# Mixture-of-experts stage: four experts at a time on 32-column tiles, in fixed order, with eight weight buffers

## What is computed

```python
N_GROUPS, EXPERTS_PER_GROUP, TOP_K, D_EXPERT = 4, 8, 2, 512
g_top_p, g_top = lax.top_k(softmax(xt @ router_group_w + router_group_b), 1)      # one group of 8 experts a token
e_logits = (xt @ router_expert_w + router_expert_b).reshape(n, 4, 8)
e_top_logit, e_top = lax.top_k(e_logits[group of the token], TOP_K)               # two experts in that group
gates = g_top_p * softmax(e_top_logit)
# for each of the token's two experts e:
hdn = silu(x @ w_gate[e]) * (x @ w_up[e])      # w_gate, w_up: 1024 x 512
y  += gate * (hdn @ w_down[e])                 # w_down: 512 x 1024
```

## Time and profile before

| | us |
|---|---|
| median of 3 runs | 2416.12 (2413.78 to 2418.14) |
| span of the profiled execution | 2417.7 |
| PE busy / weight loads / DVE / ACT / POOL | 2155.3 / 1491.3 / 746.5 / 406.8 / 186.7 |
| HBM read, written | 440.29 MB, 1.05 MB |
| mean granted TensorE clock | 0.946 |

### The profile page before, as it was taken

How to read it: one execution, slowest core, us unless ns; L and a number is a source line. 1 busy time by engine, 2 the same in 40 slices (tenths; PEclk the granted TensorE clock), 3 DMA queues, 4 the chain that set the end, 5 groups by cost and what they waited for, 6 DMA issues and landing times.

```text
span 2417.7 us, 21513 instructions
## 1 busy us (share of the span) xinstructions
PE 2155.3 (89%) x8282; PEld 1491.3 (62%) x8282; DVE 746.5 (31%) x1215; ACT 406.8 (17%) x868; POOL 186.7 (8%) x157
## 2 busy tenths in 40 slices
PE   3904999989999789999899998878999999999997
PEld 2403868777888457688788885566444444444443
DVE  4887423642232445236422233322000000000001
ACT  1112322202110242312121101331001001001001
POOL 0560300000000274000000000000000000000000
PEclk9956999999999899999999999977999999999998
DMA  7512624244446464342554465003987886886881
GB/s 270 178 69 70 207 93 153 105 163 152 148 165 226 135 231 173 106 139 105 174 166 147 144 244 172 35 1 116 335 297 247 294 307 244 296 295 244 309 294 71
DMA packets 224588, 442.54 MB, mean 183 GB/s; under 512 B 10421, under 2 KB 59765, under 8 KB 224501
## 3 DMA queue, kind: packets, MB, share of 16 engines
q1 hardware_dynamic: 221557, 440.08, 52.1%
q10 hardware_dynamic: 2944, 1.28, 0.2%
HBM read 440.29 MB, written 1.05 MB: 183 GB/s over the span
## 4 chain that ended last, share of the span: by engine, by line
PE 81%; DVE 8%; DVEq 3%; ACT 3%; issue 2%; SPq 1%; DMA 1%; ACTq 0%
PE acc L660 29%; PE acc L1092 18%; PE aux L1109 9%; PE acc L670 5%; PE acc L935 3%; PE aux L935 3%; PE acc L957 3%; PE aux L602 3%; DVE biasm L1563 2%; DVEq L1564 2%; PE acc L1038 1%; SPq L530 1%; ACT area L1144 1%; PE aux L624 1%; DVE gates L1560 1%
## 5 line engine op out<-in xcount | busy, mean ns | idle before, releaser
L660 PE MATMUL acc<-hT,ring 128*128 128x256 f32 x2688 | 594.8, 383 | 6.9 <-ACT hT L1217 6.9
L660 PEld LDWEIGHTS acc<-hT,ring 128*128 128x128 f32 x2688 | 515.3, 192 | 82.5 <-ACT hT L1217 7.7
L1092 PE MATMUL acc<-ring,area 128*128 128x512 f32 x1024 | 450.7, 594 | 3.7 <-ACT area L1144 1.9
L1092 PEld LDWEIGHTS acc<-ring,area 128*128 128x128 f32 x1024 | 192.7, 191 | 234.6 <-issue 232.7
L1109 PE MATMUL aux<-ring,area 128*128 128x512 f32 x512 | 225.4, 593 | 2.7 <-ACT area L1144 2.7
L2120 DVE SCALAR_TENSOR_TENSOR area<-area,acc 128x512 f32<-128x512 f32 x32 | 23.9, 748 | 600.0 <-PE acc L1092 600.0
L602 PE MATMUL aux<-kc,area 128*128 128x128 f32 (+2 forms) x473 | 76.7, 310 | 130.2 <-DVE area L1676 54.2
L670 PE MATMUL acc<-ring,hT 128*128 128x512 f32 (+1 forms) x384 | 167.5, 596 | 12.1 <-ACT hT L1217 12.1
L1109 PEld LDWEIGHTS aux<-ring,area 128*128 128x128 f32 x512 | 97.0, 190 | 124.2 <-issue 120.5
L602 PEld LDWEIGHTS aux<-kc,area 128*128 128x128 f32 (+2 forms) x473 | 64.3, 158 | 157.9 <-DVE area L1676 54.3
L1500 POOL TENSOR_TENSOR zb<-ring,cact 128x512 f32<-128x512 f32 x80 | 90.0, 1130 | 750.3 <-DMA ring<-in_ada_w 740.2
(11 more groups left out here) (318 smaller groups left out, 1804.5 us busy)
## 6 DMA issues: line engine op xcount, KB each, us to landing
ring<-in_w_in SPq DMA_DIRECT2D x34, 2048.0 KB, 8.9
ring<-in_w_gate SPq DMA_DIRECT2D x32, 2048.0 KB, 8.3
ring<-in_w_up SPq DMA_DIRECT2D x32, 2048.0 KB, 8.3
ring<-in_w_down SPq DMA_DIRECT2D x32, 2048.0 KB, 7.9
ring<-in_ada_w SPq DMA_DIRECT2D x28, 2048.0 KB, 9.1
ring<-in_ffn_w_up SPq DMA_DIRECT2D x44, 1024.0 KB, 7.5
ring<-in_ffn_w_down SPq DMA_DIRECT2D x10, 2048.0 KB, 8.0
ring<-in_w_out SPq DMA_DIRECT2D x6, 2048.0 KB, 7.8
```

What stands on the lines that cost most here:

```text
L660: mm = pe.matmul(acc[LU.buf[use]][:, SEQ * j:SEQ * j + SEQ], w[:, k, c0:c0 + P], x[:, k, :], start=(k == 0), stop=(k == n - 1))
L1092: mm = pe.matmul(acc[e % 2][:, DE * i:DE * i + DE], xg[:, k, :], w[:, k, :], start=(k == 0), stop=(k == KT - 1))
```

## The change

- An expert has 32 slots (`CAP`) of its own, a token has two (one for each of its experts). Four experts make a *quad*: their 4 x 32 slots fill 128 columns. PE computes the four on four column tiles: each matmul has 32 stationary columns and writes 32 partitions, and the loop runs over the four experts inside the loop over k. The matmuls of an expert run only over its own slots.
- Eight quads instead of four groups. Seven run unrolled, in fixed order; the eighth and every further pass for a quad with an expert of over 32 tokens (`overflow_table`, up to 1 + 16 passes) run in a loop whose passes and quads are read from `meta`. Each such pass loads all 12 matrices of its quad.
- Weights have eight 2 MB buffers (`slots8`: the four of `ring`, `gates` and three pieces of `area`). Eight loads are issued during the second attention. Each further load waits until the matmuls of the matrix eight before it have ended (`spent`).
- Loads put 8 (gate, up) or 4 (down) consecutive rows of a matrix on a partition, one row of 16 KB, where they put rows of 2 or 4 KB. `h2t` and `he` are copied in that order of features.
- The gate weight moves from DVE's product into the scatter matrix (`pw`). Gather, scatter and turns of neighbouring quads are placed between the batches.
- `va2`, `h2t`, `xg`, `ygs`, `fin`, `hs`, `he`, `heT` and the router's small tiles get other places, and the squares of the last two norms go to `sqx2` and `sqx3`.

```diff
-PASS_CHUNKS = ["e_g0", "e_u0"] + [...]
+W_SLOTS = 8
+RING_OF = (None, 3, 0, None, None, None, 1, 2)
+QUAD_CHUNKS = 3 * QE
+STATIC = (QUADS - 1) * QUAD_CHUNKS
+LOOP_STEP = QUAD_CHUNKS + 4
...
...
# SP
+            def expert_source(quad, c):
+                w = a[("w_gate_2", "w_up_2", "w_down_2")[c // QE]]
+                return w[0, bass.ds(quad * QE + c % QE, 1)].rearrange("e (p k) n -> p (e k n)", p=P)
+            def expert_load(n):
+                sp.dma_start(slots8[n % W_SLOTS], expert_source(n // QUAD_CHUNKS, n % QUAD_CHUNKS)).then_inc(expert_in[n % W_SLOTS], 16)
...
+                if name == "m_kb":
+                    expert_load(0)
+            mid_done("m_kb", 2)
+            expert_load(1)
+            mid_done("m_vb", 2)
+            expert_load(2)
+            sp.wait_ge(t2_out, 4)
+            expert_load(3)
+            sp.wait_ge(oT_out, 2)
+            expert_load(4)
+            expert_load(5)
+            mid_done("m_wo0", 4)
+            expert_load(6)
+            mid_done("m_wo1", 4)
+            expert_load(7)
+            for n in range(W_SLOTS, STATIC):
+                sp.wait_ge(spent, n - W_SLOTS + 1)
+                expert_load(n)
             sp.wait_ge(routed, 1)
+            passes = sp.value_load(meta[0:1, 0:1], min_val=1, max_val=1 + OVER)
+            with sp.Fori(0, passes) as i:
+                quad = sp.value_load(meta[0:1, bass.ds(i + 1, 1)], min_val=0, max_val=QUADS - 1)
+                for c in range(QUAD_CHUNKS):
+                    sp.wait_ge(spent, i * LOOP_STEP + (STATIC + c - W_SLOTS + 1))
+                    s = (STATIC + c) % W_SLOTS
+                    sp.dma_start(slots8[s], expert_source(quad, c)).then_inc(expert_in[s], 16)
...
# PE
+            def hidden(c0, b, dst, full_of):
+                for e in range(QE):
+                    full_of(c0 + e)
+                for k in range(KT):
+                    for e in range(QE):
+                        w = shaped(slots8[(c0 + e) % W_SLOTS], KT, DE)
+                        mm = pe.matmul(dst[CAP * e:CAP * e + CAP, :], xg[:, b, k, CAP * e:CAP * e + CAP], w[:, k, :],
                                        start=(k == 0), stop=(k == KT - 1))
+                        if k == KT - 1:
+                            mm.then_inc(spent, 1)
+            def down(c0, full_of, extra=0):
...
+                        for e in range(QE):
+                            w = shaped(slots8[(c0 + e) % W_SLOTS], 4, D)
+                            mm = pe.matmul(aux[CAP * e:CAP * e + CAP, 512 * n:512 * n + 512], heT[:, k, CAP * e:CAP * e + CAP],
+                                           w[:, k, 512 * n:512 * n + 512], start=(k == 0), stop=(k == 3))
+                            if k == 3 and n == 1:
+                                mm.then_inc(spent, 1 + (extra if e == QE - 1 else 0))
...
+            pe.wait_ge(pm_ready, 1)
+            gather(0, 0)
+            for q in range(QUADS - 1):
+                b, c0 = q % 2, QUAD_CHUNKS * q
+                pe.wait_ge(gx_out, q + 1)
+                hidden(c0, b, acc[b][:, 0:512], static_in)
+                if q:
...
+                    scatter(1 - b, 1 - b)
+                hidden(c0 + QE, b, acc[b][:, 512:1024], static_in)
+                if q < QUADS - 2:
...
+                    gather(1 - b, 1 - b)
+                pe.wait_ge(he_ready, q + 1)
+                turn()
+                pe.wait_ge(he_out, q + 1)
...
+                down(c0 + 2 * QE, static_in)
...
+            with pe.Fori(0, passes) as i:
...
+                gather(0, 1)
+                pe.wait_ge(gx_out, i + QUADS)
+                hidden(STATIC, 1, acc[1][:, 0:512], loop_in)
+                hidden(STATIC + QE, 1, acc[1][:, 512:1024], loop_in)
+                pe.wait_ge(he_ready, i + QUADS)
+                turn()
+                pe.wait_ge(he_out, i + QUADS)
+                down(STATIC + 2 * QE, loop_in, LOOP_STEP - QUAD_CHUNKS)
+                pe.wait_ge(yg_out, i + QUADS)
+                pe.wait_ge(pt_out, i + QUADS)
+                scatter(0, 1)
...
# ACT
-                copy(h2t[:, t, :], aux).then_inc(h2_out, 1)
+                copy(shaped(h2t[:, t, :], KT, P), aux.rearrange("p (m k) -> p k m", k=KT)).then_inc(h2_out, 1)
...
# DVE
+            tt(sel8, o1, o2nd, ALU.add)
+            D_()
+            tt(sel.rearrange("p t (g e) -> p t g e", g=GROUPS), bc(og, 3, EPG), bc(sel8, 2, GROUPS), ALU.mult)
+            D_().then_inc(og_ready, 1)
...
+            def match_slots(b, slot_of, gate_of):
+                tt(pm[:, b], bc(bc(kc[:, K_IOTA:K_IOTA + CAP], 1, QE), 1, T), bc(slot_of, 3, CAP), ALU.is_equal)
+                D_()
+                tt(pw[:, b], pm[:, b], bc(gate_of, 3, CAP), ALU.mult).then_inc(pm_ready, 1)
...
+                dve.tensor_reduce(qmax, cnt, AX, ALU.max)
+                ts(thr, row(7), float(CAP), float(CAP), ALU.mult, ALU.add)
...
+                tt(over, bc(qmax, 2, 7), bc(thr, 1, QUADS), ALU.is_gt)
...
+                dve.tensor_reduce(ext, over, AX, ALU.add)
...
+                ts(metaf[:, 0:1], cum[:, QUADS - 1:QUADS], 1.0, None, ALU.add)
...
+            match_quad(0)
+            match_quad(1)
+            overflow_table()
+            for q in range(QUADS - 1):
+                if q:
+                    add_scattered(1 - q % 2, q)
+                times_up(q % 2, QUAD_CHUNKS * q + 2 * QE, q + 1)
```

More of the change, by code:

```diff
@@ L1065, in _ @@
-            pe.wait_ge(routed, 1)
-            passes = pe.value_load(meta[0:1, 5:6], min_val=GROUPS, max_val=GROUPS + 1)
-            with pe.Fori(0, passes) as p:
-                def pass_arrived(name):
-                    s, value = PASS_RING[name]
-                    pe.wait_ge(landed[s], p * PASS_TOTAL[s] + value + MID_LANDED[s])
-                    return ring[:, s, :]
-                pe.wait_ge(pm_ready, p + 1)
+            pe.matmul(pmod[:, 256:288], tri, sel[:, 0, :], start=True, stop=True)
@@ L1113, in _ @@
[L1113 to L1125 removed]
+                transposes([(pw[:, b, t].rearrange("p e c -> p (e c)"), pmod[:, 256 + P * t:256 + P * t + P]) for t in range(T)], pt_full)
@@ new lines, in _, with loop_in @@
+            pe.wait_ge(yg_out, QUADS - 1)
+            pe.wait_ge(pt_out, QUADS - 1)
+            scatter(0, 0)
+            pe.wait_ge(routed, 1)
+            passes = pe.value_load(meta[0:1, 0:1], min_val=1, max_val=1 + OVER)
+            with pe.Fori(0, passes) as i:
+                def loop_in(n):
+                    c, s = n - STATIC, n % W_SLOTS
+                    first, per = (STATIC - s + W_SLOTS - 1) // W_SLOTS + 1 + (c >= W_SLOTS), 1 + (s >= 4)
+                    pe.wait_ge(expert_in[s], i * (16 * per) + EXPERT_BASE[s] + 16 * first)
+                pe.wait_ge(pm_ready, i + QUADS)
+                pe.wait_ge(x_added, i + QUADS - 1)
+                pe.wait_ge(pt_out, i + QUADS - 1)
+                gather(0, 1)
[9 more added lines that the diff above has]
+                scatter(0, 1)
@@ L2097, in _ @@
-            ts(metaf[:, 5:6], metaf[:, 5:6], float(GROUPS), None, ALU.add)
-            dve.tensor_copy(metaf[:, 0:GROUPS], kc[:, K_IOTA:K_IOTA + GROUPS])
-            D_()
-            dve.tensor_copy(meta[:, 0:6], metaf[:, 0:6])
-            D_().then_inc(routed, 1)
-            D_().then_inc(x_added, 1)
-            passes = dve.value_load(meta[0:1, 5:6], min_val=GROUPS, max_val=GROUPS + 1)
-            def match_slots(p):
-                for t in range(T):
-                    last = ts(pm[:, t, :], kc[:, K_IOTA:K_IOTA + P], psl[:, t, bass.ds(p, 1)], None, ALU.is_equal)
-                last.then_inc(pm_ready, 1)
@@ L2111, in _ @@
[L2111 to L2124 removed]
+            tt(psl, shaped(pmod[:, 256:320], T, EXPERTS), sel, ALU.mult)
@@ new lines, in _ @@
+            passes = dve.value_load(meta[0:1, 0:1], min_val=1, max_val=1 + OVER)
+            with dve.Fori(0, passes) as i:
+                quad = dve.value_load(meta[0:1, bass.ds(i + 1, 1)], min_val=0, max_val=QUADS - 1)
+                ts(pslr, psl[:, :, bass.ds(quad * QE, QE)], rep32[:, bass.ds(i, 1)], None, ALU.subtract)
+                dve.tensor_copy(gq, g32[:, :, bass.ds(quad * QE, QE)])
+                D_()
+                dve.wait_ge(pt_full, i + QUADS - 1)
+                match_slots(1, pslr, gq)
+                times_up(1, i * LOOP_STEP + (STATIC + 2 * QE), i + QUADS)
+                add_scattered(0, i + QUADS)
```

265 lines of the change are left out of this document (139 added, 126 removed).

## The result

The changed kernel takes 2447.39 us (median of four runs, 2445.40 to 2450.43), the kernel before 2417.13 on the same chip (2413.78 to 2420.17): 1.0118 of the time before, 95% interval 1.0093 to 1.0143. It is 30 us slower; 2447.5 was forecast. The profiled execution of the changed kernel has a span of 2443.6 us, that of before 2417.7.

The account below looks back on a forecast made before the run. PE bounds the old expert stage, weight loads the new: last static down batch ends at 2132.5 us, four spill passes add 288, the tail 28.6, giving span 2449.1; the median, 1.6 us lower, is forecast at 2447.5 us, range 2425 to 2522.

Parts of the forecast that it names:

- Four further passes, 144 matrices: Spill loop: counted assignments need four passes beyond quad 7, so 144 matrices load where 96 did, 302 MB for 201.
- rival 1: Spill loop: no spill pass runs, 2159 us; 5% together with the case of one pass more or less.
- Four tiles at a time: Expert matmuls: four column tiles run together, 6.9 us a batch at the low end, 27.5 us at the high end.
- First batch: Start of expert stage: gather from 1672.0 us, quad 0's gate batch starts at 1679.4 and ends 9 us later, 1688.4.
- Loads: Expert weights in 16 KB rows: 4.9 us a matrix, bounds 4.8 and 5.45; 88 matrices reach 2122.5 us.
- Cold batches: Expert batches after PE idles: 9 to 10 us, some 5 us at half clock; 7 at least, 14 at most.
- The pass: Each spill pass waits for the previous down batch: 72.0 us from latency, 58.8 us transfers and cold down batch; four 288.
- The tail: From the end of the last down batch to the kernel's end: stays as it was, 28.6 us.
- 5 us more in the queue are covered by idle DMA: Second attention: the first early expert load in SP's queue costs nothing; uncovered it would be 5 us.
- 3: Expert batches: two column tiles at a time, 13.8 us a batch, 2490 us; 12%.
- 4: Expert batches: tiles one at a time, 27.5 us a batch, 2874 us, or weight loads not overlapping, 2572 us; 8% for both.
- Rival 2: Weight loads: 16 KB rows gain nothing, 5.45 us a matrix, 2522 us; 17% for 5.1 us and over.

Follow-up runs that it names:

- e1: The changed kernel with loop passes set to 1, so the four spill passes and tokens beyond an expert's 32nd are left out: 2163.27 us.
- e9: Against a kernel with experts in two pairs (2453.85 us), all four experts' weights are signalled spent only with the batch's last matmul: 2483.87 us.
- e4: The changed kernel with weights loaded in rows of 2 and 4 KB instead of 16 KB, and plain copies of h2 and he: 2486.19 us.
- e2: The changed kernel with the loop over the four experts outside those over k and n, so neighbouring matmuls hit the same column tile: 2657.47 us.

## Why the prediction was right, step by step

- *Four further passes, 144 matrices.* Right: 540.95 MB of HBM reads for 541, 2304 matmuls. Counting the assignments of the inputs decided the sign. e1 shows what a miscount to none would have given, 2163 us for the 2159 of rival 1.
- *Four tiles at a time.* Right: 0.43 us for four matmuls, a warm batch of 7.07 us for the low end of 6.9. The Trainium skill, TensorE: Matmul & The Clock Gate, section on packing small matmuls, gives 2.38 times for three column tiles; it is near four times for four here (27.5 to 7.07). Its rule that a weight load overlaps running matmuls only where the row group differs, taken alone, would have made the batch some 19 us; this trace doesn't agree, since the four tiles share all rows and start within 20 ns, and the next weight loads begin 0.03 us behind the start of the first matmul. The same section also lets a weight load go ahead into the background weight buffer; the prediction left that out, and it fits this trace.
- *First batch.* The gather began 1.7 us later than put down (1673.7 for 1672.0), the batch itself 0.7 us later (1680.1 for 1679.4), since the gather was warm, 5.3 us for 6.2. The batch was warm as well, 7.07 us for 9, so it ended at 1687.2 for 1688.4. The granted clock of 0.66 that the earlier trace rows has at this place did not come again.
- *Loads.* Right: 4.87 us a matrix for 4.9, 430 GB/s. The down batch of quad 7, the last before the spill passes, ended at 2129.6 for 2132.5, 1.2 us of the difference from the first batch.
- *Cold batches.* Right: 8.5 to 10.0 us for 9 to 10; a few were warm, 7.2 us. The clock of the static part was 0.80 on average, which costs nothing there, because DMA sets the pace.
- *The pass.* 70.9, 71.3, 71.5 and 71.5 us for 72.0; the first load and its latency, transfers at full rate, a cold down batch and no overlap between passes are all seen in the chain. Four of them are 285 us for 288.
- *The tail.* 28.7 us for 28.6.
- *What failed: "5 us more in the queue are covered by idle DMA".* The text looked at PE's chunks and not at ACT, whose issue of small loads was held up behind the 2 MB: 5.2 us more of gap on ACT, 3.8 us more of wait on PE. It was priced at nothing with 5 us as the uncovered end, and the uncovered end was nearer. That the gather began only 1.7 us late is owed to the stretch between, which was 1.8 us shorter than in the trace of before.

The steps add to a span of 2449.1 us, and the trace has 2443.6, 5.5 us less: 1.2 from the first batch, 1.7 from the loads, 2.7 from the four passes. The median lay 1.6 us below the span in the kernel before, and was expected so; in the changed kernel it lies 3.8 us above the span of the profiled execution. The first difference, 5.5 us, and the sum of the other two, 5.4 us, cancel, and the agreement of 2447.5 with 2447.39 to 0.1 us is luck to that size.

Of the rivals, 3 and 4 had the right sign and the wrong price. Two tiles at a time (2490 us forecast, 2454 measured) took the whole batch to be on the path, but the first half of a batch gives its buffers back early, as e9 shows. One at a time (2874 forecast, 2657 measured) took the tiles to run strictly one after the other, but PE lets neighbours overlap. Rival 2, at 2522 us for rows that gain nothing, measured 2486 (e4), because its price came from one short window.

## What to carry to other kernels

Before a fixed order with capacities is taken for one that follows the data, count on the real inputs how often the capacity is exceeded and what one excess loads: here six (expert, level) pairs beyond 32 slots cost the weights of sixteen experts, and a list by expert turned 1.2% slower into 4.7% faster. At a seam where loads wait for buffers, look at when a batch frees them and not at how long it is; 30 us hung on that with PE doing the same work. Look as well at whether the next loads could use buffers that are free already. When a big transfer is moved into an idle queue, look at every engine that issues small transfers behind it.

## What the runs showed of the hardware

Matmuls in fp32 on four 32-column tiles start within 20 ns of each other, and the next four come 0.43 us later, the time of one instruction on all 128 columns. In an order with sixteen instructions a tile, PE still runs about the last four of a tile beside the first four of the next, that is, out of the order of the program by the starts in the record: 21.6 us for a batch and not 27.5 (e2). Whether it reaches further than four was not tried.

One core reads weights at 430 GB/s in 16 KB rows (340 us of the changed kernel) and at 406 in rows of 2 and 4 KB (380 us of e4).

A load of 2 MB in SP's queue lengthened the issue of one of ACT's small loads from 4.94 to 10.28 us when its rows were 16 KB, and to 6.42 us when they were 2 KB (e4). The Trainium skill, DMA: Bandwidth & Descriptors, section on issuing engines not being separate queues, says that transfers of all engines interleave on the same 16 DMA engines, and that issuing from several of them only saves the issue time; here the issue time itself grew, and it held up an engine on the path.
